# Paired latent keys, per-bank counts between scores and masks, preloaded square-root tables, first products whose result is unread, and stick queries in a new order

## The reference

```python
h = rmsnorm(x, norm_gain) * (1 + scale) + shift
proj = h @ w_in                    # sb_q, sb_k, sb_v, sb_z, c_q, c_kv, k_rot, mla_z, g_a, g_b
o_a = stick_breaking_attention(sb_q, sb_k, sb_v)        # 8 heads of 64
y_a = (o_a * silu(sb_z)) @ w_branch_a
q  = rmsnorm(c_q, q_norm_gain) @ w_uq                   # 8 heads, 64 plain + 32 turned
kv = rmsnorm(c_kv, kv_norm_gain) @ w_ukv                # 8 heads, 64 of keys + 64 of values
k_pe = rope(k_rot, positions)                           # one for all heads
o_b = latent_attention(q_nope, rope(q_pe), k_nope, k_pe, v_b)   # causal softmax, scale 1/sqrt(96)
y_b = (o_b * silu(mla_z)) @ w_branch_b
merged = sigmoid(g_a) * y_a + sigmoid(g_b) * y_b
out = rmsnorm(x + gate * (merged @ w_out), final_norm_gain)
```

## Time and profile before

| what | value |
| --- | --- |
| median of 3 runs | 2613.08 us (2610.19 to 2613.66) |
| profiled execution, own time | 2614.87 us |
| its span, first to last instruction | 2613.1 us |
| mean granted TensorE clock | 0.993 |
| TensorE busy | 2540.3 us, 97% |
| GpSimd busy | 1968.2 us, 75% |
| VectorE / ScalarE busy | 1075.7 us, 41% / 647.7 us, 25% |

### The profile page before, as it was taken

One profiled execution on the slowest core, in us unless ns is written; L12 is line 12 of the kernel. 1 busy time (PEld: TensorE's weight loads), 2 busy tenths in 40 slices (PEclk: granted clock), 3 DMA queues, 4 the chain that ended last, 5 costly groups with the idle time before them and its releaser, 6 DMA issues.

```text
span 2613.1 us, 48022 instructions
## 1 busy us (share of the span) xinstructions
PE 2540.3 (97%) x17482; PEld 2084.8 (80%) x17482; DVE 1075.7 (41%) x1645; ACT 647.7 (25%) x1294; POOL 1968.2 (75%) x2578
## 2 busy tenths in 40 slices
PE   8999999999999999999999999999999999999998
PEld 6888887777887888888888888678888878787767
DVE  4222038885455522211522412746444334123355
ACT  2111015653432311101211101533111013354211
POOL 8888888894325688877788877667999868756666
PEclk9999999999999999999999999999999999999999
DMA  4333322220001233333333333223444423322212
GB/s 148 101 96 97 97 85 77 81 74 4 4 4 53 80 101 96 97 97 89 93 96 96 94 96 90 64 57 105 151 144 145 123 78 103 95 63 69 87 49 85
DMA packets 119815, 226.43 MB, mean 87 GB/s; under 512 B 13424, under 2 KB 14192, under 8 KB 119664
## 3 DMA queue, kind: packets, MB, share of 16 engines
q1 hardware_dynamic: 113904, 207.22, 26.9%
q10 hardware_dynamic: 5760, 16.98, 2.0%
HBM read 222.05 MB, written 2.10 MB: 86 GB/s over the span
## 4 chain that ended last, share of the span: by engine, by line
PE 87%; issue 4%; DVE 3%; POOL 3%; ACT 2%; DMA 0%; POOLq 0%; DVEq 0%; ACTq 0%
PE bank L231 21%; PE bank L232 21%; PE bank L233 21%; PE bank L1585 1%; POOL w_lo L213 1%; PE bank L1600 1%; PE bank L270 1%; POOL w_hi L223 1%; PE bank L365 1%; PE bank L271 1%; PE bank L274 1%; PE bank L1534 1%; PE bank L2582 1%; PE bank L251 1%; PE bank L252 1%
## 5 line engine op out<-in xcount | busy, mean ns | idle before, releaser
L213 POOL TENSOR_TENSOR w_lo<-w_raw,w_hi 128x512 fp32r<-128x512 f32 x778 | 1054.6, 1356 | 63.5
L231 PE MATMUL bank<-x_hi,w_hi 128*128 128x512 f32 x1804 | 707.5, 392 | 5.0 <-POOL w_lo L213 4.9
L233 PE MATMUL bank<-x_hi,w_lo 128*128 128x512 f32 x1804 | 702.3, 389 | 0.0
L232 PE MATMUL bank<-x_lo,w_hi 128*128 128x512 f32 x1804 | 702.2, 389 | 0.0
L222 POOL TENSOR_TENSOR w_hi<-w_raw,ones 128x32 fp32r<-128x32 f32 x778 | 280.9, 361 | 382.3 <-PE bank L233 296.1
L223 POOL TENSOR_SCALAR w_hi<-w_raw 128x480 fp32r<-128x480 f32 x778 | 515.3, 662 | 0.0
L231 PEld LDWEIGHTS bank<-x_hi,w_hi 128*128 128x128 f32 x1804 | 338.7, 188 | 81.9 <-POOL w_lo L213 9.9
L233 PEld LDWEIGHTS bank<-x_hi,w_lo 128*128 128x128 f32 x1804 | 338.6, 188 | 70.4
L232 PEld LDWEIGHTS bank<-x_lo,w_hi 128*128 128x128 f32 x1804 | 338.8, 188 | 69.3 <-issue 0.2
L755 DVE TENSOR_TENSOR f<-bank,rstd 128x512 f32<-128x512 f32 x88 | 56.7, 686 | 549.3 <-PE bank L233 543.2
L231 PE MATMUL bank<-mid_hi,w_hi 128*128 128x512 f32 x656 | 255.2, 389 | 0.0
(11 more groups left out here) (511 smaller groups left out, 3663.8 us busy)
## 6 DMA issues: line engine op xcount, KB each, us to landing
w_raw<-weights SPq DMA_DIRECT2D x778, 256.0 KB, 2.6
ada_w<-ada_in ACTq DMA_DIRECT2D x24, 512.0 KB, 4.2
h<-xT ACTq DMA_DIRECT2D x8, 256.0 KB, 7.2
out<-f SPq DMA_DIRECT2D x8, 256.0 KB, 2.5
mask_b<-mask_b_in ACTq DMA_DIRECT2D x1, 640.0 KB, 4.1
spread<-spread_in SPq DMA_DIRECT2D x1, 512.0 KB, 3.7
window<-window_in ACTq DMA_DIRECT2D x1, 512.0 KB, 4.8
cond<-cond_in ACTq DMA_DIRECT2D x1, 512.0 KB, 3.4
```

What stands on the lines that cost most here:

```text
L213: pool.tensor_tensor(w_lo[:, (n - 1) % RW, :], w_raw[:, (n - 1) % RS, :], w_hi[:, (n - 1) % RW, :].bitcast(F32), ALU.subtract).then_inc(w_ ...
L231: pe.matmul(outs[m], w_hi[:, s, c], hi, start=first, stop=False)
L232: pe.matmul(outs[m], w_hi[:, s, c], lo, start=False, stop=False)
L233: done = pe.matmul(outs[m], w_lo[:, s, c], hi, start=False, stop=last)
```

## The change

1. The keys of two latent heads share one group of 128 columns: `uk` is 512 wide instead of 1024, so its first pass of two units carries all eight heads and the second pass is gone. 778 units become 776. Odd heads have their halves swapped: keys in the upper half, the turned part in the lower. So the queries of odd heads are rolled by 64 columns, a second table `turns_odd` stands beside `turns`, `rope_k` is copied for all 128 partitions, and `keys_out` writes eight tiles of 64 x 512.
2. `scores` and `masked` go through the four column groups in the order 1, 0, 2, 3 and count each group, with waits at each bank.
3. The scores of heads 1 and 2 each follow one of the two units for the values. Unit 0 of the first branch stands ahead of the third pair's values, units 1, 2 and 3 one in each of the rounds 8, 9 and 10. GpSimd splits parts 0 and 1 of `za` after divisions 4 and 5, and parts 2 and 3 after division 7.
4. The ckv projection stands in banks 2 and 3. The stick scores run in the order 0, 1, 3, 2, and only the group 2 of the first head waits for the copy of ckv.
5. `heads_low` comes ahead of the angle on DVE, the sine behind the copies of q and k on ScalarE.
6. `preload_act_table_set("sqrt_and_others")` stands behind the loads of `h` and ahead of the last squares.
7. Ten products of the constants `ident` and `ones`, whose result nobody reads, stand first on TensorE.

```diff
+        MASK_ORDER = (1, 0, 2, 3)
+        BANK_END = {1: 1, 0: 2, 3: 3}
...
-                self.n_uk = uk, uk + 5
-                self.n_uv = uk + 7
+                self.n_uk = uk
+                self.n_uv = uk + 5
...
+        CKV_AT = 2
...
+        ZA_AFTER = {4: (0,), 5: (1,), 7: (2, 3)}
...
+                        first = CKV_AT * (name == "ckv")
+                        unit_products(pe, [o[:] for o in sets[b % 2][first:first + tiles]], x_hi[:, k, :], x_lo[:, k, :], k == 0, k == KT - 1, n)
...
-            act.wait_ge(*pv("clip"))
-            act.activation(turns[:], angle[:], ACT.Sin, scale=rope_c[:, 3:4]).then_inc(*pa.tell("sin"))
             for b, (name, tiles) in enumerate(PROJ):
+                if b == 2:
+                    act.wait_ge(*pv("clip"))
+                    for j, t in enumerate((turns_odd, turns)):
+                        act.activation(t[half(j), :], angle[half(j), :], ACT.Sin, scale=rope_c[half(j), 3:4]).then_inc(*pa.tell("sin", j))
...
+            heads_low(dve)
             dve.wait_ge(tables_loaded, 64)
...
-            heads_low(dve)
...
-            pe.wait_ge(*pa("ckv", 1))
...
-                if r:
-                    pe.wait_ge(*sv("o", 2 * r - 1))
+                pe.wait_ge(*(sv("o", 2 * r - 1) if r else pa("ckv", 1)))
...
-                for t in range(TT):
+                for t in (0, 1, 3, 2):
+                    if a == 0 and t == 2:
+                        pe.wait_ge(*pa("ckv", 0))
                     pe.matmul(at(t), stick_k[a][:, t * P:(t + 1) * P], stick_q[a][:, t * P:], start=t != 3, stop=False, skip_group_check=True)
...
-            pe.wait_ge(*lv("turns_q"))
+            pe.wait_ge(*lv("turns_odd"))
...
             pe.wait_ge(*lv("q", 3))
-            latent_keys(pe, s, 0, sb_)
+            latent_keys(pe, s, sb_)
             pe.wait_ge(*pa("gb1", 3))
...
-            act.activation(mla_k[half(1), :, :], rope_k[half(1), :].rearrange("p (a t) -> p a t", a=1).to_broadcast([64, HEADS_B, T]), ACT.Copy).then_inc(*la.tell("k"))
+            for j in two:
+                r = half(1 - j)
+                act.activation(of_parity(mla_k, j)[r], rope_k[r, :].rearrange("p (a t) -> p a t", a=1).to_broadcast([64, HEADS_B // 2, T]),
+                               ACT.Copy).then_inc(*la.tell("k", j))
...
+            dve.tensor_tensor(turns_odd[:], turns_odd[:], sb_[1][:], ALU.mult).then_inc(*lv.tell("turns_odd"))
+            dve.wait_ge(*lv("turns_odd"))
             queries_out(dve, s, 0)
...
             for m in range(4):
-                dve.tensor_tensor(mla_k[half(0), 4 * b + m, :], bank[(SETB, SETA)[b]][m][half(0), :], rstd[half(0), :], ALU.mult).then_inc(*lv.tell("k", 4 * b + m))
+                for j in two:
+                    dve.tensor_tensor(mla_k[half(j), 2 * m + j, :], bank[SETB][m][half(j), :], rstd[half(j), :], ALU.mult).then_inc(*lv.tell("k", 2 * m + j))
...
             def scores(a):
-                if a:
-                    pe.wait_ge(*mv("mask", a - 1))
-                for n in range(TT):
+                for n in MASK_ORDER:
+                    if a and n in BANK_END:
+                        pe.wait_ge(*mv("mask", a - 1, BANK_END[n]))
                     c = LATENT_AT[n]
-                    done = pe.matmul(columns(s_bank, c, c + (n + 1) * P), mla_q[:, a, n * P:(n + 1) * P], mla_k[:, a, 0:(n + 1) * P], start=True, stop=True)
-                done.then_inc(*mp.tell("score", a))
+                    pe.matmul(columns(s_bank, c, c + (n + 1) * P), mla_q[:, a, n * P:(n + 1) * P], mla_k[:, a, 0:(n + 1) * P],
+                              start=True, stop=True).then_inc(*mp.tell("score", a, n))
...
-            pe.wait_ge(*lv("k", 3))
-            pe.wait_ge(*la("k"))
+            pe.wait_ge(*lv("k", 7))
+            pe.wait_ge(*la("k", 1))
             scores(0)
             pe.wait_ge(*lv("q", 7))
-            latent_keys(pe, s, 1, bank[SETA])
-            scores(1)
-            pe.wait_ge(*lv("k", 7))
             for k in range(2):
                 moving_units(pe, bank[SETA], ckv_hi, ckv_lo, k, 2, s.n_uv + k)
-            scores(2)
+                scores(1 + k)
             pe.wait_ge(*la("v", TT - 1))
             for i in ROUNDS:
                 for a in head_at(i, 0):
                     if a >= 3:
                         scores(a)
+                if i == HEADS_B:
+                    pe.wait_ge(*mv("mask", HEADS_B - 1, MASK_ORDER[-1]))
+                    branch_unit(pe, s, 0, 0)
                 for r in pair_at(i):
                     values(r)
                 for a in head_at(i, 2):
                     turned_scores(a)
-                if i >= HEADS_B + 1:
-                    for k in ((0,), (1, 2), (3,))[i - HEADS_B - 1]:
-                        branch_unit(pe, s, 0, k)
+                if HEADS_B <= i < HEADS_B + 3:
+                    branch_unit(pe, s, 0, i - HEADS_B + 1)
...
-                dve.wait_ge(*mp("score", a))
                 if a >= 3:
                     dve.wait_ge(*mp("turn", a - 3))
-                for n in range(TT):
+                for n in MASK_ORDER:
+                    if n in BANK_END:
+                        dve.wait_ge(*mp("score", a, BANK_END[n]))
                     c = LATENT_AT[n]
                     e = c + (n + 1) * P
...
+                dve.wait_ge(*mv("mask", a, MASK_ORDER[-1]))
...
-                if i == 0:
-                    keys_out(dve, s, 1)
...
-            for a in range(4):
-                divide(a)
-            pool.wait_ge(*sv("o", 7))
-            pool.wait_ge(w_used, s.n_a)
-            for k in range(4):
-                divide(4 + k)
+            def stick_parts(k):
                 pool.tensor_scalar(za_hi[:, k, :], sb_z[:, k, :], 1.0, 0.0, ALU.mult, ALU.add).then_inc(*mg.tell("hi", k))
                 pool.wait_ge(*mg("hi", k))
                 pool.tensor_tensor(za_lo[:, k, :], sb_z[:, k, :], za_hi[:, k, :].bitcast(F32), ALU.subtract).then_inc(*mg.tell("lo", k))
+
+            for a in HEADS_AT:
+                divide(a)
+                if a == 4:
+                    pool.wait_ge(*sv("o", 7))
+                    pool.wait_ge(w_used, s.n_a)
+                for k in ZA_AFTER.get(a, ()):
+                    stick_parts(k)
...
+            act.preload_act_table_set("sqrt_and_others")
             for k in each:
...
+            act.preload_act_table_set("sqrt_and_others")
...
+            for _ in range(10):
+                pe.matmul(bank[SETA][3][:, 0:P], ident[:], ones[:], start=True, stop=True)
             ffn_tensor(pe, f0)
...
-    uq = np.concatenate([uq, swap(uq[..., 64:])], 2).reshape(384, D)
+    uq = np.concatenate([uq, swap(uq[..., 64:])], 2).reshape(384, HEADS_B // 2, 2, P)
+    uq = np.stack([uq[:, :, 0], np.roll(uq[:, :, 1], 64, -1)], 2).reshape(384, D)
     ukv = i["w_ukv_2"][0].reshape(256, HEADS_B, 128)
-    uk = np.concatenate([ukv[..., :64], none(ukv, 64)], 2).reshape(256, D)
+    uk = ukv[..., :64].reshape(256, 512)
```

More of the change, by code:

```diff
@@ L2329, in program @@
         stick_l = [table(f"stick_l{j}", [P, TRI]) for j in range(2)]
+        turns_odd = table("turns_odd", [P, T])
         stick_hi, stick_lo = (sb(n, [P, TRI], F32R, at=where["gate_b"] + 4 * TRI * j) for j, n in enumerate(("stick_hi", "stick_lo")))
@@ L2519, in second_vector @@
             step("clip", "phase", angle, angle[:], PI, -PI, ALU.min, ALU.max)
-            dve.wait_ge(*pa("sin"))
-            dve.memset(turns[0:64, :], 1.0).then_inc(*pv.tell("one"))
+            dve.wait_ge(*pa("sin", 1))
+            for j, t in enumerate((turns, turns_odd)):
+                dve.memset(t[half(j), :], 1.0).then_inc(*pv.tell("one", j))
             dve.memset(less_ones[:], -1.0).then_inc(stick_ones, 1)
```

59 lines of the change are left out of this document (29 added, 30 removed).

## The result

The changed kernel takes 2591.8 us in the median of four runs (2587.77 to 2594.4), the kernel before 2613.3 (2610.19 to 2613.66). The ratio is 0.9919 with an interval of 0.9902 to 0.9936. The direction of the forecast is right, and the time is 0.7 us under the lower end of its range. The profiled execution took 2592.23 us with a span of 2590.4, so 22.7 us of span are gone where the sum said 17.7. I went through the stages in the order of the forecast, each against the rows of before.

A forecast was written before the change was run, and what follows sets the result against it. It took TensorE to bound the kernel, with 87% of the span hanging on it. Terms of 2.0 + 1.1 + 6.1 + 1.7 + 5.5 + 1.3 = 17.7 us gave a median of 2595.4 us, range 2592.5 to 2602.5.

The forecast's parts named there:

- start: First branch: earlier table load and ten idle products bring TensorE's work forward until GpSimd bounds it; 2.0 us (0.8 to 2.6).
- stick scores: Ahead of the stick scores: TensorE's 1.18 us wait for the ckv copies goes; 1.1 us (0 to 1.2).
- to the first transposition: Latent attention: without the second key pass, values and divisions come earlier; 6.1 us (5.0 to 6.9).
- rounds: Latent rounds: counts per bank remove the scores' wait, two rounds take 9.3 for 9.96 us; 1.7 us (0 to 2.0).
- last rounds: After the last latent mask: branch units fill TensorE's gaps; 5.5 us (2.8 to 6.0).
- end: Before the last root: the table load moves into a wait ahead of the squares; 1.3 us (0 to 1.3).
- The middle of the projections: Projections: sine and low parts change places, with small extra pieces; nothing gained, 0 to 0.5 us as a loss.
- A: Latent attention keeps its pace, DVE bounding rounds; last rounds gain 2.8, start 0.8; sum 12.1 us, 2601.0; chance 0.27.
- B: Latent attention: removed products were cover, the softmax chain sets the transpositions; only 4.4 us remain, 2608.7; chance 0.06.
- C: Slower: the granted clock falls in the latent attention and stays low; 2647 us; chance 0.02.
- D: More gain: GpSimd less disturbed at the start, gap at the transposition closes; sum 19.6 us, 2593.5; chance 0.07.

The follow-up runs named there:

- the kernel without both edits: Changed kernel without the ten idle products and without the early table load at the start: 2594.61 us (5 runs).
- the first comparison: Changed kernel, all edits, against the kernel before: 2591.8 us (four runs) against 2613.3, ratio 0.9919.
- the first chip: Changed kernel run again, beside the kernel before and versions with start edits alone or undone: 2593.84 us against 2610.95, ratio 0.9938.
- on the second: Second chip, changed kernel run again beside its filled version and the kernel before: 2594.91 us against 2613.52.
- the kernel before, filled: Kernel before plus idle products in TensorE's waits at 470 us (6) and the change of block (15): 2609.8 us, ratio 0.9987.
- the filled version: Changed kernel with 12 idle products instead of 10 at the start, 15 at the change of block, 6 at 470 us: 2590.08 us, again 2590.05.

## Why the forecast came out as it did

The traces bear out the mechanism of every term, and the sizes within 0.5 us:

| term | forecast | traces |
| --- | --- | --- |
| start | 2.0 (0.8 to 2.6) | 1.5; 2.1 against the kernel without both edits; 0.7 to 1.1 where the clock did not rise |
| stick scores | 1.1 | 1.0 by the gap, 1.2 by the stage |
| to the first transposition | 6.1 | 6.2 |
| rounds | 1.7 | 2.1 |
| last rounds | 5.5 | 5.3 |
| end | 1.3 | 1.3 |
| sum | 17.7 | 17.4 to 18.2 |

The start's bound by GpSimd held (27.34 for the end of its rest, forecast "about 27.1"). The middle of the projections cost nothing. The rounds gained 0.4 more. The forecast took TensorE's busy time of 9.27 as what it needs; without a gap it needs 9.01. The busy time before holds the end of the transposition ahead of each gap (1.28 us shown, where in the changed kernel the next product starts 1.13 behind its start) and 0.10 us more for the scores behind it. The counts carry more than the forecast gave them: 3.6 us when taken out alone, for 1.7. Of the rivals, A (DVE keeps the pace) is out by the rounds, and B by the key pass put back. C asked for the lower level to hold, and the clock was 1.00 all through the stage. D would have needed the gap ahead of the transposition to close; it stayed at 0.98.

The step that failed is under the sum: "The median of the runs is 1.8 us below that execution, so I forecast 2595.4 for the median". I carried the profiled execution over with one constant, and treated the rest of the span as the same in both kernels. In that part the clock falls at some places and not at others, at 1.71 us of pace each: five times in the profiled execution of the kernel before, two to four times in the four of the kernels that have all edits of the second block on the first comparison and the first chip. And TensorE's waits between 578 and 809 us vary by as much again. So the difference of two small samples moves by several microseconds, which a range of 3 us below the forecast did not hold. The range had no term for it: it was said to come from one term at a time at its bound, and for 2593.5 to 2598.5 that gives 2594.6 (6.9 for 6.1) to 2598.1 (2.8 for 5.5). The 14 runs of the changed kernel, in three comparisons, have a median of 2593.4 us (2587.77 to 2598.01), and 59 of the kernel before 2612.8 (2607.11 to 2618.53). By those the change is worth 19.4 us and its time lies inside the range. The four runs of the first comparison were on the low side; the difference was 21.5 us there, 17.1 on the first chip and 18.6 on the second.

What stays open: the span times (1 - mean clock), that is the pace that the falls take, is 14.0 us in the mean of 55 runs of before and 9.8 in the 14 of the changed kernel. The fall in the last rounds, which the sum had, is 1.7 of the 4.2. Some 0.8 are no time at all: in every profile the record has the lower level once more behind TensorE's last product (from 2605.99, the product having ended at 2605.22), and there it takes 3.9 to 4.6 us in the three profiles with all of the old end and 3.4 to 3.6 in the three of the changed kernel. Whether the change makes the other falls a little rarer, or the rest of 1.7 is chance, these runs don't settle: kernels that differ from it in one or two places had 10.4 and 11.4 on the first chip and 11.3 to 15.6 on the second. Nor is that pace the time: in the kernel before, filled, it is 6.9 us instead of 14.1, and the median is only 4.0 us shorter.

## What to carry to other kernels

Before a sum of saved waits becomes a time, look for what differs from run to run in the parts that the change does not touch. Here the granted clock in windows of 5 us and the idle time of an untouched stretch show it; both belong in the range. Several executions profiled beforehand would size it, as one does not. In this kernel waits of 1.9 to 3.3 us were often followed by a fall of the clock, which cost 1.6 us more in the last rounds and less where another engine held the pace; idle products in such waits are cheap where their bank is free. Before such a filler is valued, ask what comes late once the stretch behind it runs at full pace: in the old order VectorE's sequence took 1.5 us of it.

## What was not expected of the hardware

- While TensorE has products to run, every fall of the granted clock in the fourteen profiles has one size: 0.50 for 3.4 us (1.71 us of pace), or twice that at the change of block. At 470 it comes 0.4 to 1.2 us after TensorE has resumed: in the kernel before the gap ends at 471.75, and the products turn from 0.39 to 0.63 us at 472.9.
- The length of the wait alone does not decide. Gaps of 2.02 to 2.10 us at 470 had a fall in eight of eleven profiles, and gaps of 2.49 and 2.01 in the last rounds in two of three profiles of that order.
- The same ten idle products from 1.72 us on raised the clock ahead of the first real product in four profiled executions and did not in four others (0.47 or 0.76 us for that product). The twelve of the filled version did in both of its profiles. The Trainium skill (TensorE: Matmul & The Clock Gate, Part 1) says that the moment of the rise varies from run to run; the traces agree. Unit 8 starts at 30.2 to 30.4 us in the four where it rose in time and at 30.8 to 31.1 in the others, so the rise is worth 0.4 to 0.9 us, where the forecast had 1.2 (2.0 less 0.8).
